# Decay logarithms spread over the opening's blocks, and GpSimd making five of eight low halves of a norm's first part

## The reference

```python
for l in range(DEPTH):
    sh1, sc1, g1, sh2, sc2, g2 = split(silu_c @ w_mod[l] + b_mod[l], 6)
    log_decay = jax.nn.log_sigmoid(ret_decay_logit[l])
    hx = rmsnorm(x) * (1 + sc1) + sh1            # norm n1_l (ctx likewise, with its own six)
    y_x = token_mixers(hx @ w_in[l], log_decay[0], log_decay[1], st_f, st_b, mix_conv_w[l], rope)
    x = x + g1 * (y_x @ w_out[l])
    x = x + g2 * conv_ffn(rmsnorm(x) * (1 + sc2) + sh2, ...)   # norm n2_l
return rmsnorm(x, final_norm_g)
```

## Time and profile before

| | us |
|---|---|
| median of 3 runs | 1617.33 (1615.39 to 1617.8) |
| the profiled execution's own time | 1619.17 |
| its span, first to last instruction | 1617.4 |
| TensorE busy in it | 1559.5 |
| VectorE, GpSimd, ScalarE busy | 919.3, 888.8, 331.7 |

### The profile page before, as it was taken

One profiled execution on the slowest core, in us unless ns is written; L12 is line 12 of the kernel. 1 busy time (PEld: TensorE's weight loads), 2 busy tenths in 40 slices (PEclk: granted clock), 3 DMA queues, 4 the chain that ended last, 5 costly groups with the idle time before them and its releaser, 6 DMA issues.

```text
span 1617.4 us, 24334 instructions
## 1 busy us (share of the span) xinstructions
PE 1559.5 (96%) x8962; PEld 1325.4 (82%) x8962; DVE 919.3 (57%) x1367; ACT 331.7 (21%) x512; POOL 888.8 (55%) x830
## 2 busy tenths in 40 slices
PE   7989999999999999999999999999998999999997
PEld 5778888887788888888888888877778888888886
DVE  3876444498887865873378646454545441341444
ACT  3602111311312101120021224111223220220221
POOL 2264333475455565654565544554464776777764
PEclk7999999999999999999999999999999999999999
DMA  8453111244234343332333323231222323233223
GB/s 333 146 168 100 58 40 40 89 154 145 92 130 130 110 142 115 128 130 77 106 125 109 105 80 100 82 92 53 66 78 66 104 93 100 92 99 108 91 91 105
DMA packets 50082, 172.63 MB, mean 107 GB/s; under 512 B 6241, under 2 KB 8801, under 8 KB 48993
## 3 DMA queue, kind: packets, MB, share of 16 engines
q1 hardware_dynamic: 46080, 165.70, 30.6%
q10 hardware_dynamic: 3936, 6.06, 1.3%
HBM read 165.44 MB, written 2.10 MB: 104 GB/s over the span
## 4 chain that ended last, share of the span: by engine, by line
PE 64%; DVE 22%; issue 7%; ACT 3%; DMA 2%; POOL 1%; DVEq 1%; ACTq 1%; SPq 0%
PE pair L1251 51%; DVE aux L737 6%; PE pair L1359 5%; DVE tg L1189 3%; DVE tv L1189 3%; DVE hid_lo L1217 1%; DVE tv L1214 1%; ACT tv L707 1%; ACT hid_hi L715 1%; PE aux L1569 1%; DMA raw<-in_slabs 1%; PE aux L1539 1%; PE aux L1640 1%; DVE h_lo L883 1%; DVE mod_acc L737 1%
## 5 line engine op out<-in xcount | busy, mean ns | idle before, releaser
L446 POOL TENSOR_SCALAR w_hi<-raw 128x512 fp32r<-128x512 f32 (+1 forms) x412 | 298.5, 725 | 674.3 <-PE pair L1251 530.7
L448 POOL TENSOR_TENSOR w_lo<-raw,w_hi 128x512 fp32r<-128x512 f32 (+1 forms) x412 | 592.0, 1437 | 34.4
L1251 PE MATMUL pair<-h_hi,w_hi 128*128 128x512 f32 x1760 | 530.7, 359 | 13.9 <-DVE tv L1189 5.0
L1251 PE MATMUL pair<-h_lo,w_hi 128*128 128x512 f32 x1760 | 523.5, 355 | 1.6 <-DVE h_lo L1091 1.4
L1251 PE MATMUL pair<-h_hi,w_lo 128*128 128x512 f32 x1760 | 521.7, 354 | 0.0
L1251 PEld LDWEIGHTS pair<-h_hi,w_hi 128*128 128x128 f32 x1760 | 288.6, 189 | 66.5 <-issue 13.1
L1251 PEld LDWEIGHTS pair<-h_lo,w_hi 128*128 128x128 f32 x1760 | 288.8, 189 | 51.1 <-DVE h_lo L1091 3.1
L1251 PEld LDWEIGHTS pair<-h_hi,w_lo 128*128 128x128 f32 x1760 | 288.6, 189 | 45.9
L737 DVE CUSTOM_DVE_ANT_0 aux<-mod_slot,c_b 128x1024 f32<-128x1024 f32 x160 | 234.8, 1467 | 4.8 <-DMA mod_slot<-in_mods 2.1
L1144 DVE SCALAR_TENSOR_TENSOR x<-pair,modv,x 128x256 f32 (+3 forms) x84 | 53.0, 658 | 169.0 <-PE pair L1251 168.8
L1251 PE MATMUL pair<-hid_hi,w_hi 128*128 128x512 f32 x486 | 146.8, 356 | 0.2 <-POOL w_lo L448 0.2
(11 more groups left out here) (177 smaller groups left out, 1329.6 us busy)
## 6 DMA issues: line engine op xcount, KB each, us to landing
raw<-in_slabs SPq DMA_DIRECT2D x206, 512.0 KB, 3.5
mod_slot<-in_mods SPq DMA_DIRECT2D x80, 512.0 KB, 3.5
start_slot<-in_start_mods SPq DMA_DIRECT2D x8, 1024.0 KB, 15.4
x<-in_x SPq DMA_DIRECT2D x4, 768.0 KB, 9.6
rot<-kT ACTq DMA_DIRECT2D x32, 64.0 KB, 2.0
rot<-Y ACTq DMA_DIRECT2D x32, 64.0 KB, 2.1
out<-fin SPq DMA_DIRECT2D x16, 128.0 KB, 1.9
c_b<-in_c SPq DMA_DIRECT2D x1, 512.0 KB, 7.6
```

The lines of the kernel that those rows point to most:

```text
L446: nc.gpsimd.tensor_scalar(w_hi[p][:, a:b], raw[p][:, a:b], 1.0, 1.0, ALU.mult, ALU.mult).then_inc(split, 1)
L448: nc.gpsimd.tensor_tensor(w_lo[p][:, a:b], raw[p][:, a:b], w_hi[p][:, a:b].bitcast(fp32), ALU.subtract).then_inc(split, 1)
L1251: ins = nc.tensor.matmul(out[:, a:b], wt, xt[:, a:b], start=first and k == 0, stop=last and k == 2)
```

## The change

1. `log_decays(block)` is called from within the first norm, after `scale(k + 1)` and ahead of `low(k)`: two operations at block 0, three at block 2, three at block 3, two each at blocks 4, 5 and 6, three at block 7. Its exponential goes into ScalarE's loop, behind block 1 and the copy of start rows that follows it.
2. In `n2_0`, `n1_1` and `n2_1`, part 0, the blocks k = 3 to 7 (`DVE_LOWS = 3`) take another way: ScalarE adds the shift in place in `nt`, waits for that, and copies `nt` to `h_hi`; GpSimd subtracts h_hi from nt into `h_lo`. VectorE's `low` is left out there, and `scale(0, k)` waits for GpSimd instead for k = 5 to 7. GpSimd does these five between the splits of the pair's own two slabs and that of the next slab.
3. In `pair_behind_norm` the lag of the second slab in part 1 goes from 1 to 5.

```diff
+DVE_LOWS = 3
+def low_ready(norms, pool_low, name, part, k):
+    if part == 0 and k >= DVE_LOWS:
+        return pool_low, (KB - DVE_LOWS) * NORMS.index(name) + k - DVE_LOWS + 1
+    return norms[name]["h_ready"], (DVE_LOWS if part else 0) + k + 1
...
+            def lows(name):
+                _, a, b = norm_parts(name)[0]
+                for k in range(DVE_LOWS, KB):
+                    pool.wait_ge(norms[name]["hi_ready"], k + 1)
+                    nc.gpsimd.tensor_tensor(h_lo[:, k, a:b], nt[k % 2][:, a:b], h_hi[:, k, a:b].bitcast(fp32), ALU.subtract)\
+                        .then_inc(pool_low, 1)
+            behind = {PLAN[0, "up", 0] + 2: "n2_0", PLAN[1, "kv"] + 2: "n1_1", PLAN[1, "up", 0] + 2: "n2_1"}
             for s in range(PLAN["end"]):
+                if s in behind:
+                    lows(behind[s])
                 for half in range(2):
                     split_half(s, half)
...
                     if name == "n1_0" and k + 3 < KB:
                         move_start_rows(k + 3)
+                    if name == "n1_0" and k == 1:
+                        act.wait_ge(ld_ready, 1)
+                        nc.scalar.activation(ldt[:, 0, :], ldt[:, 1, :], ACT.Exp, scale=-1.0).then_inc(ld_ready, 1)
...
                 def high(part, k):
                     st, a, b = parts[part]
                     act.wait_ge(s["nt_ready"], KB * part + k + 1)
+                    if part == 0 and k >= DVE_LOWS:
+                        nc.scalar.activation(nt[k % 2][:, a:b], nt[k % 2][:, a:b], ACT.Identity, bias=mod(l, st, sh, k))\
+                            .then_inc(shifted, 1)
+                        act.wait_ge(shifted, (KB - DVE_LOWS) * NORMS.index(name) + k - DVE_LOWS + 1)
+                        nc.scalar.activation(h_hi[:, k, a:b], nt[k % 2][:, a:b], ACT.Copy).then_inc(s["hi_ready"], 1)
+                        return
...
+                    if name == "n1_0":
+                        log_decays(k)
                     for st, a, b in cols:
                         dve.wait_ge(s["hi_ready"], len(cols) * k + st + 1)
...
                 for k in range(1, KB):
                     if k + 1 < KB:
                         scale(0, k + 1)
-                    low(0, k)
+                    if k < DVE_LOWS:
+                        low(0, k)
                     if k == 3:
                         invert(1)
...
-                for part, lag in ((0, 3), (1, 1)):
+                for part, lag in ((0, 3), (1, 5)):
```

More of the change, by code:

```diff
@@ L305, in build_program @@
              for n in ["n1_0"] + NORMS}
+    pool_low, shifted = sem("h_low_by_gpsimd"), sem("shift_added")
     for k in ("sums_done", "rs_ready", "rinv_ready", "rbc_ready"):
@@ L587, in _ @@
                     norm("n1_0", TC, 0, SH1, lambda k: act.wait_ge(x_loaded[k // 2], 16))
-                    act.wait_ge(ld_ready, 1)
-                    nc.scalar.activation(ldt[:, 0, :], ldt[:, 1, :], ACT.Exp, scale=-1.0).then_inc(ld_ready, 1)
                 else:
@@ L755, in _, with log_decays @@
             dve.wait_ge(fills, 2)
-            def log_decays():
+            def log_decays(block):
                 lg = vecs[:, vec_at["logit"]:vec_at["logit"] + DEPTH * 24]
                 ya, yb, yc = ldt[:, 0, :], ldt[:, 1, :], ldt[:, 2, :]
-                chain(nc.vector.tensor_scalar(yb, lg, -1.0, None, ALU.mult))
-                nc.vector.tensor_tensor(yb, yb, lg, ALU.max).then_inc(ld_ready, 1)
-                dve.wait_ge(ld_ready, 2)
-                chain(nc.vector.tensor_scalar(yb, ya, 2.0, None, ALU.add))
-                chain(nc.vector.reciprocal(yb, yb))
-                chain(nc.vector.tensor_tensor(ya, ya, yb, ALU.mult))
-                chain(nc.vector.tensor_tensor(yb, ya, ya, ALU.mult))
-                chain(nc.vector.tensor_scalar(yc, yb, 1.0 / 17, None, ALU.mult))
-                for k in range(15, 1, -2):
-                    chain(nc.vector.scalar_tensor_tensor(yc, yc, 1.0 / k, yb, ALU.add, ALU.mult))
-                chain(nc.vector.scalar_tensor_tensor(yc, yc, 1.0, ya, ALU.add, ALU.mult))
-                chain(nc.vector.tensor_scalar(yb, lg, 0.0, None, ALU.min))
-                nc.vector.scalar_tensor_tensor(ld[:, :], yc, -2.0, yb, ALU.mult, ALU.add).then_inc(ld_ready, 1)
@@ new lines, in series @@
+                def series(first, last):
+                    for k in range(first, last, -2):
+                        chain(nc.vector.scalar_tensor_tensor(yc, yc, 1.0 / k, yb, ALU.add, ALU.mult))
+                if block == 0:
+                    chain(nc.vector.tensor_scalar(yb, lg, -1.0, None, ALU.mult))
+                    nc.vector.tensor_tensor(yb, yb, lg, ALU.max).then_inc(ld_ready, 1)
+                elif block == 2:
+                    dve.wait_ge(ld_ready, 2)
+                    chain(nc.vector.tensor_scalar(yb, ya, 2.0, None, ALU.add))
+                    chain(nc.vector.reciprocal(yb, yb))
+                    chain(nc.vector.tensor_tensor(ya, ya, yb, ALU.mult))
+                elif block == 3:
+                    chain(nc.vector.tensor_tensor(yb, ya, ya, ALU.mult))
+                    chain(nc.vector.tensor_scalar(yc, yb, 1.0 / 17, None, ALU.mult))
+                    series(15, 13)
+                elif block == 4:
+                    series(13, 9)
+                elif block == 5:
+                    series(9, 5)
+                elif block == 6:
+                    series(5, 1)
+                elif block == 7:
+                    chain(nc.vector.scalar_tensor_tensor(yc, yc, 1.0, ya, ALU.add, ALU.mult))
+                    chain(nc.vector.tensor_scalar(yb, lg, 0.0, None, ALU.min))
+                    nc.vector.scalar_tensor_tensor(ld[:, :], yc, -2.0, yb, ALU.mult, ALU.add).then_inc(ld_ready, 1)
@@ L875, in scale @@
                     if k > 1:
-                        dve.wait_ge(s["h_ready"], KB * part + k - 1)
+                        dve.wait_ge(*low_ready(norms, pool_low, name, part, k - 2))
                     nc.vector.scalar_tensor_tensor(nt[k % 2][:, a:b], aux(2 + part)[:, 0:b - a], mod(l, st, sc, k),
@@ L949, in _ @@
                     norm("n1_0", TC, 0, SC1, SH1)
-                    log_decays()
                 def rope(buf, unit):
@@ L1421, in ready @@
                 def ready(part, n):
-                    return (s["hi_ready"], KB * part + n + 1), (s["h_ready"], KB * part + n + 1)
-                for part, lag in ((0, 3), (1, 1)):
+                    return (s["hi_ready"], KB * part + n + 1), low_ready(norms, pool_low, name, part, n)
+                for part, lag in ((0, 3), (1, 5)):
                     for p, k in in_turns(KB, lag):
```

## The result

The changed kernel takes 1622.8 us (median of 20 runs, 1617.0 to 1628.3), the kernel before in the same rounds 1617.6 (20 runs, 1611.9 to 1624.7). The ratio is 1.0027, 95% interval 1.0014 to 1.0039: 4.4 us slower (the two medians themselves lie 5.2 apart). The prediction had given no change that can be told 0.47 and slower 0.37; slower came. The forecast of 1620.1 was 2.7 us too low; the first rival's 1621.8, with the clock falling in the opening, was nearer, and its mechanism is what the trace shows. The profiled execution took 1626.54 with a span of 1624.8, 7.4 above before's span.

The account below looks back on a forecast made before the run. TensorE, busy 96% of the span, was taken to bound the kernel. Opening 0.7, `n2_0` 1.6, `n1_1` 0.5 and `n2_1` 0 sum to +2.8 us, median 1620.1; own range 1618.5 to 1621.8, stated range 1614.3 to 1623.3.

Parts of the forecast that it names:

- the first rival: Opening: clock falls behind the hole before block 2, costing 1.7; opening +2.4, sum 4.5, time 1621.8; chance 0.27.
- The opening's delay: Block 2 of the first norm: load and exponential cost TensorE 1.5 us uncovered, plus 0.5 waiting for VectorE's steps.
- The opening's sum: Opening up to `ring_mods`: start about 69.5 instead of 68.80, so +0.7 us, bounds -1.4 and +2.4.
- the steps costed "at nothing": Opening, blocks 0 and 2 to 5: logarithm steps, at most 0.75 us a block, lie in VectorE's waits for ScalarE.
- the 1.3 us that `ring_mods` was to get back: Opening behind the key's copy: of VectorE's 8.6 us of logarithms, at most 1.4 to be had.
- `n2_0`: Second norm's pair: part 0 ends 2.0 late, the slabs behind go on at 427.0 instead of 425.34, +1.6 us.
- The second rival: Faster: TensorE soaks up the load, clock stays up behind `n2_0` with a 1.7 us hole; -3.4, 1613.9; chance 0.17.
- `n1_1`: Part 0 costs nothing; part 1's late VectorE meets lag 5 with nearly no hole: +0.5 us, between -0.3 and +1.5.
- `n2_1`: Later norm's pair: late low halves and four tiles moved into the 1.89 us hole cancel: 0, between -0.6 and +1.0.

Follow-up runs that it names:

- logs only: Kernel before with only the logarithms spread over the opening's blocks and the exponential with its table load behind block 1's start-rows copy; norms as before: 1624.2 us, ratio 1.0030.
- load only: Kernel before plus one dummy one-column exponential behind block 1's start-rows copy, bringing the table load there; logarithms stay behind the norm: 1622.4 us, ratio 1.0013.
- four activations: Kernel before plus four unused ScalarE activations, about 1.7 us in all, ahead of block 2's first h_hi, no table load moved: 1625.0 us, ratio 1.0031.
- three loads: Whole change plus a dummy exponential and a dummy square root ahead of the real exponential in block 1, against the kernel before: 1625.6 us, ratio 1.0038.
- swapped kernels: Six kernels with the exponential before block 1's start-rows copy, four with the whole change, two with spread logarithms alone; ratios to the kernel before 0.9989 to 1.0019.

## Why the prediction was right and wrong

- **The opening's delay: right.** Load and exponential stand behind the start rows, cover nothing, and TensorE stood 1.96 us. The wait of 0.5 for VectorE came as forecast, though block 6's two steps alone make it. `rope` waits for its transfers.
- **The opening's sum: the failed step.** "I take +0.7" left the clock's fall out of the sum, as a rival at 0.27. All five traced kernels with a delayed h_hi, with or without a table load, have the product behind the hole at half clock (0.90 to 1.01 us a pair instead of 0.62), and none of the nine others (both traces of the kernel before included) has the hole; in four of the five the hole is the likely cause, logs only can't tell. By blocks, with the spread taken off, the load costs 4.1 - 0.3 = 3.8: 1.56 of hole and 2.2 of clock. Two smaller terms were off too: the steps costed "at nothing" at blocks 2 to 5 cost 0.3, and of the 1.3 us that `ring_mods` was to get back behind the key's copy only 0.95 came, since `rope`'s first operation waited for GpSimd (1.66 instead of 0.68). So the opening is 3.8 + 0.3 + 0.5 - 0.95 = +3.65 against one in the same clock, not +0.7. The rival's +2.4 let the clock cost 1.7; by the same count it cost 2.6 in load only, 2.5 with four activations and 1.4 with three loads. The argument against the rival was that this hole is shorter than the 3.0 us one behind `n2_0`. Holes of 1.92 to 2.42 us here were followed by half clock just the same.
- **`n2_0`: mechanism right, size off.** +0.76, forecast +1.6. Part 0 was 1.5 late instead of 2.0: a trip of two blocks takes 414.57 - 410.98 = 3.59 us, where 3.7 was worked out, since the copy is 0.63 and not 0.72 and GpSimd's low 1.27 and not 1.30. That makes about half of the difference. From part 1's start to the slabs it is 429.64 - 421.26 = 8.38 us instead of 425.34 - 416.22 = 9.12, 0.7 less where 0.4 less was worked out: VectorE met GpSimd at both ends of part 1, as weighed (1.23 and 1.27 against 0.48), and still finished in time for all but 0.45 us. And the term isn't one number: at a low clock it has the other sign (table of the norms).
- **The second rival** wanted the clock to stay up behind `n2_0` with a hole of 1.7. In the change's trace the hole came (1.72) and the clock fell. Over all traces the clock fell behind the hole of 3.15 in six of eight, behind that of 1.72 in two of six, so the rival had something, though not a gain that the runs show. Its sum of -3.4 also leaves out `n1_1`'s +0.5.
- **`n1_1` and `n2_1`.** `n2_1` came at +0.3 (forecast 0): from its product at 1244.74 to the slabs at 1261.37 it is 16.63, before 16.37. In `n1_1` the offset between the two traces fell by 1.1 where +0.5 was forecast, but in before the clock was low there for 6.8 us, in after for half as long. At the same clock, from the table, it is +0.6 to +1.0 (3.4 us low), and +1.9 where the clock stays full.
- **The sum.** With the change's own clock it is 3.65 + 0.8 + 0.6 to 1.0 + 0.3 = 5.3 to 5.7, beside 4.4 by the ratio (2.3 to 6.3) and 5.2 by the medians. Most of it is in the opening: swapping two instructions gives 0.9997. That the time lay inside the stated range is due to the first rival, whose case is what happened; the main forecast's own 1618.5 to 1621.8 missed it.

What stays open: four of the six swapped kernels had another half-clock stretch from about 44 or 45 us on without a long hole (their three blocks are 13.28), and none of the three traces without spread logarithms and without delay had it (11.73, 11.74, 11.74). In the four the clock had come up at 40.8 us or later, in the other two at 39.1, so one trace each can't part the spread from the moment at which the clock rises. Whether the 0.07 to 0.16 us by which the spread lengthens each block has to do with it was not tested; if so, it costs 1.25 us in some executions.

## What to carry to other kernels

Idle time of an engine covers only what is queued ahead of the wait, not behind it: put a table load before the instruction that waits, never between it and the result that the bottleneck needs. Price a new hole of TensorE at the hole plus the products at the lower clock behind it; here 1.6 us of delay cost 3.8 by the blocks. Compare two traces place by place with a control of the unchanged kernel, since two executions of one kernel differed here by 3.9 us, and compare only places where the clock was low for as long: the same edit in `n2_0` costs 0.8 us at full clock and saves 1.4 at the lower one.

## What the hardware showed that I had not expected

TensorE ran its saturated products at two steady rates at full clock. In layer 0's first MLP group, two splits on GpSimd that are 96 products of 768 columns apart, in the kernel before, in the same kernel again, and in the change:

```profile
464.78 0.62 POOL L446 TENSOR_SCALAR w_hi<-raw 128x512 fp32r<-128x512 f32 x1 [0.99 <-PE pair L1251]
...
498.06 0.62 POOL L446 TENSOR_SCALAR w_hi<-raw 128x512 fp32r<-128x512 f32 x1 [0.99 <-PE pair L1251]
```

```profile
463.79 0.62 POOL L446 TENSOR_SCALAR w_hi<-raw 128x512 fp32r<-128x512 f32 x1 [1.31 <-PE pair L1251]
...
497.70 0.62 POOL L446 TENSOR_SCALAR w_hi<-raw 128x512 fp32r<-128x512 f32 x1 [1.31 <-PE pair L1251]
```

```profile
469.76 0.62 POOL L458 TENSOR_SCALAR w_hi<-raw 128x512 fp32r<-128x512 f32 x1 [1.32 <-PE pair L1299]
...
503.68 0.62 POOL L458 TENSOR_SCALAR w_hi<-raw 128x512 fp32r<-128x512 f32 x1 [1.31 <-PE pair L1299]
```

33.28 us is 347 ns a product, 33.91 and 33.92 are 353. The first trace of the kernel before kept 347 through that group and the change 353, which is 2.4 of the 7.4 us between their traces; but the unchanged kernel's second trace is at 353 too, and of the other eleven kernels of the table five were at 347 there and six at 353. With the norms as before it is four of seven traces at 353, with the norms changed four of seven as well. So this goes by chance and is no cost of the change. What sets the rate was not found.
